# Expert weights of the third bank that fill free scratch are asked for before the units that wait for the output projection

## What is computed

```python
    for i in range(DEPTH):
        mod = cond @ ada_w[i] + ada_b[i]
        ...
        h = modulate(rms_norm(x, norm_mix[i]), sh_m, sc_m)
        ...            # y = diff_attention(h, ...) or mla_attention(h, ...), each ends in "@ w_o"
        x = x + g_m[:, None, :] * y
        h = modulate(rms_norm(x, norm_ffn[i]), sh_f, sc_f)
        x = x + g_f[:, None, :] * hier_moe(h, ...)

    # hier_moe, for all experts e: w1, w3 (1024 x 256), w2 (256 x 1024)
        hid = jax.nn.silu(a) * b * combine[:, g, :, None]     # a = t @ w1, b = t @ w3
        out = out + jnp.einsum('nef,efd->nd', hid, w2[g])
```

## Time and profile before

| | us |
|---|---|
| time, median of 3 runs | 1208.34 (1208.19 to 1208.75) |
| the profiled execution's own time | 1204.86 |
| span of the profiled execution | 1203.1 |
| PE busy | 1049.4 (87%) |
| DVE busy | 617.6 (51%) |
| DMA, mean over the span | 277 GB/s |

### The profile page before, as it was taken

The page is one execution under the profiler, slowest core; times in us unless marked ns, Lnnn a source line. Parts: engine busy times, 40 slices in busy tenths (PEclk is TensorE's granted clock), DMA queues, the critical chain, the costliest instruction groups (busy, mean ns, idle before and its releaser), DMA issues.

```text
span 1203.1 us, 15221 instructions
## 1 busy us (share of the span) xinstructions
PE 1049.4 (87%) x5596; PEld 631.3 (52%) x5596; DVE 617.6 (51%) x1477; ACT 328.9 (27%) x909; POOL 95.1 (8%) x124
## 2 busy tenths in 40 slices
PE   2799999897998799978678999899899799988885
PEld 2344444455557556645445656555456666655552
DVE  6999699787336422212227477777334532212225
ACT  3411111577211121111113454566222111111110
POOL 1000000000000111111100000000000121111202
PEclk9999999999998899989989999999998899989999
DMA  9877876404918699999987500110605799999996
GB/s 376 326 283 308 349 281 256 179 1 173 386 70 339 257 415 419 418 418 418 419 335 293 200 28 1 36 71 1 279 36 224 292 401 421 419 419 418 418 420 268
DMA packets 63183, 333.04 MB, mean 277 GB/s; under 512 B 10679, under 2 KB 10935, under 8 KB 31745
## 3 DMA queue, kind: packets, MB, share of 16 engines
q1 hardware_dynamic: 46928, 291.39, 60.0%
q0 software_dynamic: 13968, 33.44, 7.2%
q10 hardware_dynamic: 2208, 7.18, 1.6%
HBM read 316.71 MB, written 33.05 MB: 291 GB/s over the span
## 4 chain that ended last, share of the span: by engine, by line
PE 59%; DVE 17%; DMA 12%; issue 5%; ACT 4%; SPq 3%; DVEq 0%; ACTq 0%; POOLq 0%
PE PP L740 15%; PE PP L660 9%; PE PP L755 7%; DMA ring<-in_moe_w 5%; PE PP L551 4%; PE PP L859 3%; DVE AHS L1352 3%; PE PP L575 3%; SPq L468 3%; DMA RQK<-in_moe_w 2%; PE PP L901 2%; PE PP L725 2%; DVE ring L1352 2%; PE PP L905 2%; PE PP L612 2%
## 5 line engine op out<-in xcount | busy, mean ns | idle before, releaser
L551 PE MATMUL PP<-ring,AHS 128*128 128x512 f32 x384 | 169.1, 597 | 7.3 <-DMA ring<-in_da_w_qkv 7.3
L1658 DVE TENSOR_TENSOR PS<-PS,PP 128x256 f32<-128x256 f32 x33 | 13.9, 421 | 208.6 <-PE PP L740 197.9
L551 PEld LDWEIGHTS PP<-ring,AHS 128*128 128x128 f32 x384 | 72.3, 192 | 92.2 <-issue 92.2
L660 PE MATMUL PP<-ring,AHS 128*128 128x512 f32 x256 | 113.1, 601 | 0.8 <-ACT AHS L1196 0.8
L1665 DVE SCALAR_TENSOR_TENSOR PS<-PP,small,GF 128x512 f32<-128x512 f32 x66 | 46.5, 746 | 113.3 <-PE PP L755 113.3
L740 PE MATMUL PP<-RQK,RV 128*64 128x256 f32 x768 | 90.4, 393 | 13.6 <-issue 7.7
L740 PE MATMUL PP<-ring,RV 128*64 128x256 f32 (+1 forms) x672 | 82.8, 389 | 10.0 <-issue 5.2
L740 PEld LDWEIGHTS PP<-RQK,RV 128*64 128x64 f32 x768 | 66.2, 142 | 40.4 <-issue 24.7
L740 PE MATMUL PP<-AHS,RV 128*64 128x256 f32 x640 | 74.9, 392 | 7.5 <-issue 7.5
L660 PEld LDWEIGHTS PP<-ring,AHS 128*128 128x128 f32 x256 | 48.9, 193 | 60.0 <-issue 60.0
L740 PEld LDWEIGHTS PP<-ring,RV 128*64 128x64 f32 (+1 forms) x672 | 62.3, 144 | 33.2 <-issue 12.4
(11 more groups left out here) (314 smaller groups left out, 1568.5 us busy)
## 6 DMA issues: line engine op xcount, KB each, us to landing
RQK<-in_moe_w SPq DMA_DIRECT2D x72, 1024.0 KB, 22.1
ring<-in_moe_w SPq DMA_DIRECT2D x63, 1024.0 KB, 19.0
AHS<-in_moe_w SPq DMA_DIRECT2D x60, 1024.0 KB, 25.9
ring<-in_ada_t SPq DMA_DIRECT2D x24, 1024.0 KB, 4.9
AHS<-in_ada_t SPq DMA_DIRECT2D x24, 1024.0 KB, 21.2
ring<-in_da_w_qkv SPq DMA_DIRECT2D x12, 1024.0 KB
y_d<-GF POOLq DMA_DIRECT2D x2, 4096.0 KB, 30.4
AHS<-y_d ACTq DMA_DIRECT2D x6, 1024.0 KB, 6.9
```

The lines of the kernel that those rows point to most:

```text
L551: last = mm(PB[n % 4][:, :], HT[:, c, t * P:(t + 1) * P], us[c // 4][:, (c % 4) * NH:(c % 4 + 1) * NH], start=c == 0, stop=c == C - 1)
L660: last = mm(PB[2 * t + n][:, :], (OT, OTM)[l][:, k, t * P:(t + 1) * P], us[k // 2][:, (k % 2) * D + n * NH:(k % 2) * D + (n + 1) * NH], st ...
```

## The change

In each layer, SP's list is put into another order for pairs 1 and 2. Which slots of `ring` hold `w_o` is worked out as `projecting` (k = 2 to 5 in both layers). Layer 0 asks for k = 4 and 5 of pair 2 before those four units; layer 1 asks for k = 0, 1, 4 and 5 of pair 2 before them. In layer 1 the slots of k = 0 and 1 of pair 2 now wait for `omla` (all attention output stored) and no longer for `mla_kv`, which comes earlier. No other engine's list is changed, nor is any size.

```diff
             def free_projected(l, k):
 
                 if k < 2:
-                    sp.wait_ge(*((sem("mla_kv"), 4 * T) if l else (sem("wo"), 2 * T)))
+                    sp.wait_ge(*((sem("omla"), 8) if l else (sem("wo"), 2 * T)))
                 elif k < 4:
                     sp.wait_ge(sem("lg"), T * (l + 1))
                 else:
...
-                for n in range(BETWEEN):
-                    experts(l, n, (4, 5, 0, 1, 2, 3) if n == BANKS - 1 else range(6))
+                projecting = [k for k in range(6) if moe_holder[l][(first_slot[l] + k) % RING][0] == "wo"]
+                experts(l, 0)
+                experts(l, 1, [k for k in range(6) if k not in projecting])
+                experts(l, 2, (0, 1, 4, 5) if l else (4, 5))
+                experts(l, 1, projecting)
+                experts(l, 2, (2, 3) if l else (0, 1, 2, 3))
+                for n in range(BANKS, BETWEEN):
+                    experts(l, n)
```

## The result

The changed kernel took 1194.55 us (median of 4 runs, 1192.70 to 1195.42), the kernel before 1208.26 us beside it (4 runs). The ratio is 0.9899, 95% interval 0.9873 to 0.9925: faster by 12.2 us, between 9 and 15. Where the kernel before was run more often, its medians were 1206.55 (21 runs), 1206.65 (18) and 1205.74 (12), so the 1208.3 from which the forecast subtracts was itself some 2 us high.

A forecast was written before the change was run, and what follows sets the result against it. It took the start of PE's first step, held by the first gather, as the bound; 3.5 + 2.4 + 0.9 + 0.85 + 0.8 = 8.45 us off 1208.3 gave 1199.9, range 1196.3 to 1204.6.

The forecast's parts named there:

- What bounds the kernel: Expert stages: the full weight stream starts when PE has used pair 0's w1; the first gather holds PE's first step.
- The naive 15 us for six earlier units: Expert stages: each unit fetched earlier worth 2.54 us of stream, two in layer 0, four in layer 1; turned down.
- The first gather: Pair 0's rows, each layer: shorter prefetch burst lets them land sooner; PE starts 3.5 us earlier in layer 0, 2.4 in layer 1.
- The clock term of the first matmuls: First 64 matmuls of each layer's first step: half the clock loss comes back, 0.85 and 0.8 us.
- The transposes' 0.9 us: Layer 0's eight transposes: with less idle time ahead, 0.9 us won from 1.96 us, bounds 0 and 0.9.
- The rival that the clock doesn't help in the matmuls: First matmuls take 8.5 us again, as transposes don't count for the clock: gain 6.8, time 1201.5; chance 0.30.
- The early DMAs: Units issued early delay the filling of `y_d` at most 5.1 us, to 335.4, with 34 us of cover: cost 0.
- no gain in layer 0: The burst isn't what slows layer 0's first gather, so layer 0 yields nothing: 1205.1; chance 0.08.
- no gain at all: The stream is the bound and gives the gain back, since the same bytes must pass: 1208.3; chance 0.08.
- a loss: Layer 0's early units push `y_d` filling and `xn_d` writes past the gather's start: 1216 at 55 us delay; chance 0.04.

The follow-up runs named there:

- the held-back units: Kernel before, with the units the change asks for early (two in layer 0, four in layer 1) asked for late instead: 1201.00 us, ratio 0.9934.

## Why the prediction was wrong, point by point

**What bounds the kernel: right.** Behind the release the stream neither gives the gain back nor adds to it: release to the first weights of the next layer is the same within 1.5 us in layer 0, and release to the output within 1.1 us in layer 1, over the profiles of all kernels whose units aren't held back. The naive 15 us for six earlier units were rightly turned down, though the measured 12.2 look like them; the held-back units show that the gain has another cause.

**The first gather: right in kind, and nearly in size.** Layer 1 was to gain 2.4 us at PE's start and gained 2.5; the gather landed after 4.2 us instead of the 3.4 assumed, but PE was busy longer anyway. Layer 0 was to gain 3.5 and gained 2.5 (4.01 us of idleness gone, less the 1.6 us by which the idle multiplications took 6.80 instead of 5.18 us): the clock fell in them this time.

**The clock term of the first matmuls: this is the step that failed.** The transposes' 0.9 us came. For the first 64 matmuls the prediction took half of 1.7 and 1.6 us, 1.65 in all, on the reason that a gap of 1.8 us remained ahead of them. The pair of profiles gave 1.5 and 1.4, together 2.9; that is all there was to win in that execution, since the first step takes 7.13 us at full clock and not the 6.91 of the later step from which the 1.7 and 1.6 were counted. And the loss was taken from a single execution in which it was small: first matmul to release 5.2 and 5.1 us, where the other layers with the old list and 22 idle multiplications had 6.5 twice in layer 0, and 6.3 and 6.6 in layer 1.

Over the three profiles with the old list in a layer and the three with the new one, the first matmuls bring 1.8 us in layer 0 and 2.3 in layer 1, 4.1 instead of 1.65. PE's earlier start brings 6.4 instead of 5.9. Gather to release goes from 18.41 to 12.50 us in layer 0 and from 17.51 to 11.93 in layer 1, 11.5 us together, near the timed 12.2; but these are six executions, one of them the longest of its twelve, and no average of either kernel. The forecast's sum was 3 us short of that, most of it the matmuls' term, and the 1208.3 from which it was taken lay 2 us above what more runs of before gave. Both errors put the forecast too high; together they make the 5.3 us between 1199.9 and 1194.55. The range couldn't hold the result either: even all its terms at their largest gave 1196.1.

**The rival that the clock doesn't help in the matmuls: wrong in the changed kernel's own profiles**, four of four first steps at 3.70 us or a hundredth more. The eight transposes and the gap of 1.8 us stand ahead of fast and slow first matmuls alike, so they alone don't decide it. But half was not a foolish weight: with the new list in layer 0 alone, with the held-back units and with 14 idle multiplications, the clock fell in the first matmuls of layer 0 all the same (5.39 us each time). In the kernel with layer 0 alone the granted clock shows it, just behind 391.42, where the matmuls began (columns as in the earlier trace rows):

```profile
391.80:395.00 3.20, 3.20 (x18) 2.23 (x16) 2.82 (x12) 0.67 (x1) 0.00 (x0) 0.50 0.24 65
```

In each of these the idle multiplications had run at full clock (22 of them in 5.18 us, or 14 in 3.39). Wherever they had taken longer (6.80, or 5.02 for 14) and PE then waited 1.1 us or less for the gather, the first matmuls ran at full clock; in layer 1 of the first profile of before they had taken 6.80 too, but 2.37 us of waiting followed, and the matmuls were slow. The reverse doesn't hold: in layer 1 with the new list there alone (22 in 5.18 us), and with 14 (3.39 us, then 1.55 us of waiting), the first matmuls ran at full clock too. In most of these first steps there is a stretch at half clock, and what it costs depends on whether it falls into work that nobody waits for; what sets its moment stays open.

**The early DMAs: right.** The filling of `y_d` ended 4.9 us later (335.20), within the 5.1 allowed, and no later step felt it. The rivals of no gain in layer 0, of no gain at all and of a loss are out by the kernel with layer 0 alone and by the result.

**The 3.8 us outside** the two stretches were scatter between executions as far as the repeats tell: up to the first gather of layer 0 the unedited profiles of both kernels have 385.6 to 387.7, the latents 29.9 to 32.3. The prediction had no term for such scatter of the clock; its range was made of bounds of the terms alone.

## What to carry to other kernels

A stream that runs at its full rate doesn't make every earlier byte worth its share: find the event that starts the stream, and ask what holds that event. A small transfer on the critical path that meets a burst of prefetch pays for the burst; moving part of the burst ahead of it, where the DMA engines have time to spare, takes the price away without a debt later. Take a clock loss from several executions before sizing a term by it, and give a gap that remains ahead of heavy matmuls some idle multiplications.

## What the runs showed of the hardware

A gather of 128 rows of 4 KB took 3.1 to 3.5 us from issue to landing with no other DMA beside it (3.7 and 4.6 once each, in the kernels with the 6 added idle multiplications), 4.2 us with a second one 1.4 us behind it, 8.3 to 10.1 us beside a burst of ten weight units of 1 MB, and 11 to 12 us at some places in the full stream.

The same program's executions differ: 1202.1 to 1210.9 us for the kernel before in one set of 12, with a mean granted clock of 0.975 in the fastest and 0.967 in the slowest, and 22 idle multiplications took 5.18 us or 6.80 us. The median of these 12 runs lay 0.22% below that of 21 others of the same program.
